# Attention in a hybrid layer: turned units rounded ahead of the exponentials, keys and values of a pair made in the shortest steps

## What is computed

```python
q = (rms_norm(c_q, q_norm_g) @ w_uq).reshape(B, S, 8, 64 + 32)       # then rope on the last 32
kv = (rms_norm(c_kv, kv_norm_g) @ w_ukv).reshape(B, S, 8, 64 + 64)   # k_nope, v; k_rope is shared by the heads
s = (einsum('bqhd,bkhd->bhqk', qn, k_nope) + einsum('bqhr,bkr->bhqk', qr, k_rope)) * scale
mask = key_chunk[None, :] <= q_chunk[:, None]                        # chunks of 64 positions
p = softmax(where(mask, s, -inf), axis=-1)
out = einsum('bhqk,bkhd->bqhd', p, v)
```

## Time and profile before

| | us |
|---|---|
| median of three runs (lowest to highest) | 2465.4 (2462.1 to 2468.1) |
| the profiled execution, its own time | 2465.6 |
| its span, first to last instruction | 2463.4 |
| PE busy in the span | 2246.3 |
| DVE busy | 1623.0 |
| ACT busy | 1220.3 |

### The profile page before, as it was taken

One profiled execution on the slowest core, in us unless ns is written; L12 is line 12 of the kernel. 1 busy time (PEld: TensorE's weight loads), 2 busy tenths in 40 slices (PEclk: granted clock), 3 DMA queues, 4 the chain that ended last, 5 costly groups with the idle time before them and its releaser, 6 DMA issues. The chain is left out here.

```text
span 2463.4 us, 42754 instructions
## 1 busy us (share of the span) xinstructions
PE 2246.3 (91%) x13522; PEld 1897.7 (77%) x13523; DVE 1623.0 (66%) x2948; ACT 1220.3 (50%) x2007; POOL 364.3 (15%) x255
## 2 busy tenths in 40 slices
PE   7999999998898999989979995899999999999970
PEld 6999989896777777777868885777777788888760
DVE  5445454556778778777756786687786765656646
ACT  4333333324666666666642220565665654454536
POOL 0000000000100001000001111123242322323216
PEclk9999999998999999999989996899999999999995
DMA  4122111251000000000134434698989978978837
GB/s 177 61 84 82 65 60 60 91 180 47 6 5 16 7 6 17 5 8 10 41 132 153 159 130 154 235 355 302 364 313 353 334 222 278 314 217 263 309 86 280
DMA packets 157242, 368.34 MB, mean 150 GB/s; under 512 B 25792, under 2 KB 37824, under 8 KB 155200
## 3 DMA queue, kind: packets, MB, share of 16 engines
q1 hardware_dynamic: 142592, 318.88, 35.5%
q0 software_dynamic: 13104, 47.72, 7.9%
q10 hardware_dynamic: 1440, 0.37, 0.1%
HBM read 295.11 MB, written 72.35 MB: 149 GB/s over the span
## 5 line engine op out<-in xcount | busy, mean ns | idle before, releaser
L2029 PE MATMUL eH<-w_hi,at_tok 128*128 128x512 f32 x720 | 288.8, 401 | 11.0 <-DVE at_tok L2147 11.0
L2080 ACT CAST w_hi<-w_raw 128x4096 fp32r (+1 forms) x64 | 232.7, 3636 | 109.6 <-DMA w_raw<-in_w 75.8
L2030 PE MATMUL eH<-w_hi,at_tok 128*128 128x512 f32 x720 | 286.3, 398 | 0.0
L2089 DVE TENSOR_TENSOR w_raw<-w_raw,w_hi 128x4096 f32 (+1 forms) x64 | 282.6, 4416 | 0.2 <-issue 0.2
L1224 DVE TENSOR_TENSOR prT_lo<-pT,prT_hi 128x512 fp32r<-128x512 f32 (+1 forms) x288 | 189.4, 658 | 97.6 <-ACT prT_hi L1104 97.5
L2089 DVE TENSOR_TENSOR w_raw<-w_raw,at_row 128x4096 f32 x32 | 141.6, 4426 | 125.1 <-ACT at_row L2080 125.0
L1104 ACT CAST prT_hi<-pT 128x512 fp32r<-128x512 f32 (+1 forms) x288 | 162.7, 565 | 120.6 <-PE pT L1008 119.9
L1142 POOL TENSOR_TENSOR qT_lo<-q_raw,qT_hi 128x512 fp32r<-128x512 f32 x32 | 41.0, 1280 | 1155.8 <-ACT qT_hi L1086 1155.8
L1215 DVE TENSOR_REDUCE mx<-pS 128x1 f32<-128x512 f32 (+2 forms) x320 | 188.5, 607 | 6.4 <-PE pS L998 1.2
L2034 PE MATMUL eH<-w_raw,at_tok 128*128 x720 | 183.9, 397 | 8.7 <-DVE w_raw L2089 8.6
L1096 ACT ACTIVATE pr<-pS,nmx 128x512 f32<-128x512 f32 (+1 forms) x240 | 154.0, 645 | 71.7 <-DVE nmx L1219 71.2
(11 more groups left out here) (369 smaller groups left out, 5680.6 us busy)
## 6 DMA issues: line engine op xcount, KB each, us to landing
w_raw<-in_w SPq DMA_DIRECT2D x96, 2048.0 KB, 13.8
xt<-in_x SPq DMA_DIRECT2D x9, 1024.0 KB, 8.1
xs<-in_x SPq DMA_DIRECT2D x8, 1024.0 KB, 5.1
scratch_h<-hp SPq DMA_DIRECT2D x16, 512.0 KB, 2.7
scratch_z<-hp SPq DMA_DIRECT2D x16, 512.0 KB, 3.6
fz<-scratch_z SPq DMA_DIRECT2D x16, 512.0 KB, 8.1
out<-fz SPq DMA_DIRECT2D x16, 512.0 KB, 2.6
scratch_xT<-xT_hi SPq DMA_DIRECT2D x7, 1024.0 KB, 3.9
```

The costliest lines, as they stand in the source:

```text
L2029: pe.matmul(H[:], xh[:, k, :], w.hi[:, k, :], start=(k == 0), stop=False)
L2030: pe.matmul(H[:], xl[:, k, :], w.hi[:, k, :], start=False, stop=False)
L2080: nc.scalar.copy(w.hi[:], w.words(o).bitcast(F32)).then_inc(w.hi_ready, 1)
L2089: v.tensor_tensor(w.words(o), w.words(o).bitcast(F32), w.hi[:].bitcast(F32), ALU.subtract).then_inc(w.lo_ready, 1)
```

## The change

Four edits, all in `phase_b` and its tables.

1. On ScalarE a half rounds two turned units (slots 0 and 1) before its first exponential, and from then on the casts run one ahead of the exponentials. Before, each cast was followed by an exponential.
2. Keys and values of the next pair are made in steps 14, 15 (of the odd head) and 0, 1 (of the pair's own even head): "k" in each first half, "v" in each second half, chunk 0 to 3.
3. Where the pieces and the preparations of a half are at most four together (`prep_leads`), the preparations come ahead of the slots: on PE right behind the scores, on VectorE right behind the maximum, on ScalarE behind the first exponential. This holds for all key and value chunks (those of pair 0 in steps 0 to 2 too) and for the query chunks of steps 1, 3, 5, 11, 13 and 15, not for those of 7 and 9.
4. The lo part of the very first query chunk is made by VectorE in the prologue and not by GpSimd.

```diff
-V_STEPS = {(3, 0): 0, (4, 1): 1, (6, 1): 2, (7, 0): 3}
+PAIR_STEPS = {(NQ + 6, 0): [("k", 0)], (NQ + 6, 1): [("v", 0)], (NQ + 7, 0): [("k", 1)], (NQ + 7, 1): [("v", 1)],
+              (0, 0): [("k", 2)], (0, 1): [("v", 2)], (1, 0): [("k", 3)], (1, 1): [("v", 3)]}
 
 
 def prep_in(n, i):
 
-    h, turn = STEPS_B[n][0], n % NQ
     out = list(FIRST_STEPS.get((n, i), []))
-    if h % 2 == 1 and h + 1 < HEADS:
-        if i == 0 and turn % 2 == 0:
-            out.append(("k", h + 1, turn // 2))
-        if (turn, i) in V_STEPS:
-            out.append(("v", h + 1, V_STEPS[turn, i]))
+    pair = (n + NQ) // (2 * NQ) * 2
+    if 0 < pair < HEADS:
+        out += [(kind, pair, c) for kind, c in PAIR_STEPS.get((n % (2 * NQ), i), [])]
...
+def prep_leads(n, i):
+
+    return PIECES[n][i] + len(prep_in(n, i)) <= 4
...
                         if n < NI:
                             score(n, i)
+                            if prep_leads(n, i):
+                                for p in prep_in(n, i):
+                                    project(p)
                         for s in slots_in(n, i):
...
-                        if n < NI:
+                        if n < NI and not prep_leads(n, i):
                             for p in prep_in(n, i):
                                 project(p)
...
-                        for k in range(max(len(slots), pieces)):
+                        for k in range(max(len(slots), pieces + 1)):
                             if k < len(slots):
                                 if slots[k] < NU:
                                     cast(slots[k])
                                 if slots[k] in COPY_SLOT:
                                     copy_o(COPY_SLOT[slots[k]])
-                            if k < pieces:
-                                exp(n, i, k)
-                            if k == 0 and n < NI:
+                            if 1 <= k <= pieces:
+                                exp(n, i, k - 1)
+                            if k == 1 and n < NI:
                                 for p in rounding:
                                     round_q(p)
+                                if prep_leads(n, i):
+                                    for p in prep_in(n, i):
+                                        copy(p)
                         if n < NI:
-                            for p in prep_in(n, i):
-                                copy(p)
+                            if not prep_leads(n, i):
+                                for p in prep_in(n, i):
+                                    copy(p)
...
-                for no in range(NQC):
+                pool.wait_ge(q_lo, 1)
+                for no in range(1, NQC):
...
                 for p in PROLOGUE:
                     ready(p)
+                    if p == q_chunk(0):
+                        v.wait_ge(q_hi, 1)
+                        v.tensor_tensor(ql[:, 0], qst[:, 0], qh[:, 0].bitcast(F32), ALU.subtract).then_inc(q_lo, 1)
                 for n in range(NI + 2):
                     for i in range(2):
                         if n < NI:
                             peak(n, i)
+                            if prep_leads(n, i):
+                                for p in prep_in(n, i):
+                                    ready(p)
```

More of the change, by code:

```diff
@@ L966, in project @@
                     at = slice(c * 512, (c + 1) * 512)
-                    if c == 0 and x == 0 and kind == "k":
+                    if c == 0 and x == 0:
                         pe.wait_ge(w_loaded[g], h // 4 * 48 + 48)
```

## The result

The changed kernel takes 2481.1 us in the median (2480.1 to 2483.8, four runs), the kernel before 2464.8 (2462.1 to 2468.1). The ratio is 1.0067 with a 95% interval of 1.005 to 1.0085: slower by 16 us. The forecast was 2480 us.

A forecast was written before the change was run, and what follows sets the result against it. It took a ring of waits among the in-order queues of PE, ACT and DVE to bound the attention stage. Terms -29 - 18 + 42 + 16 + 3 - 0.4 = +14 on 2465.6 gave 2480 us, range 2457 to 2500.

The forecast's parts named there:

- The short steps: Steps 30 to 33, which take in keys and values: 35.7 us where it was 20.2; +14 a pair, +42 us for three.
- the chain: In one half, maximum, exponential, copy, split of keys or values and splits of units follow one another; the next maximum waits behind.
- The 2.2 us for casts behind PE's projections: Step 14, key half: two casts wait for turns that stand behind the key matmuls on PE, 2.2 us on top of 5.6.
- Keys and values out of the long steps: Steps 40 to 45 and their like lose five key and value chunks: 6.1 us a pair, -18 us for three.
- The 7.0 of the windows: Steps 40 to 45 against 56 to 61: 10.5 us less, 3.5 of it two query chunks, the rest 7.0.
- The casts: Two casts before the first exponential: 0.4 us gained in each of 72 halves, -29 us.
- Leading query chunks: Query chunks ahead of the slots in steps 3, 5, 11, 13: +4 for each 16 steps, +16 us.
- Steps 0 to 2: Same chunks in the changed order, units on top of the chain in four halves and one more exponential: +3 us.
- First query chunk: POOL's subtraction of 1.28 becomes one of 0.7 on DVE, with the first maximum behind it: -0.4 us.
- The chain overlaps after all: Rival: copies early enough that DVE pays only its own work, short steps 5.8 a pair; 2439 us, chance 0.16.
- Casts worth twice as much: Rival: a half gains 0.6 to 0.7 and the sum is within 5 us of zero; 2467 us, chance 0.14.
- The clock: Rival: PE's clock falls in the emptier short steps, +4 us a pair; 2492 us, chance 0.18.

The follow-up runs named there:

- copies-first run: The changed kernel, but ACT copies leading keys and values at the very start of the half, before casts and exponential: 2439.6 us, ratio 0.9907.
- the move alone: Edits 2 and 4 on the kernel before; preparations at the end of a half, casts and exponentials in turns: 2472.2 us, ratio 1.0031.
- queries behind: The changed kernel, but a half that makes queries does its preparations at its end: 2468.5 us, ratio 1.0016.
- the lead: Edits 3 and 4 on the kernel before, with old places and old order of casts and exponentials: 2504.0 us, ratio 1.0164.
- casts first in the old places: The changed kernel with the old places of keys and values (edits 1, 3 and 4): 2520.7 us, ratio 1.0236.
- casts and the move: The changed kernel without edit 3, every preparation at the end of its half: 2451.3 us, ratio 0.9954.

## Why the prediction was right, point by point

**The short steps** were the heart and held: 35.7 us forecast, 36.4 measured. By halves: forecast 7.8, 4.0, 3.9, 4.3, 4.4, 2.9, 4.3, 4.1; measured 8.3, 3.8, 4.2, 4.4, 4.3, 2.9, 4.6, 4.0. What made this exact was that steps 0 to 2 of the kernel before already ran the chain, so that nearly each link had a row. The 2.2 us for casts behind PE's projections had none: it was an estimate, and in the trace the second cast ends 2.7 us after the maximum. I also expected DVE to wait 1 to 1.3 us in each half; it was 0.99 to 1.51 in seven and 4.28 in the first. That what stands ahead of the copy is the cost, and not something of the same size, is shown by the copies-first run.

**Keys and values out of the long steps:** forecast -6.1 a pair, measured -7.4 with the move alone. The 7.0 of the windows was nearer; I took off too much for query chunks.

**The casts** were mis-sized: -29 forecast, -16 measured. The 0.4 us a half is right only in the last head (steps 56 to 61: 5.1 us in their twelve halves). In the falling heads that also make keys and values it is 0.3 (steps 24 to 29: 3.5 us), and in the rising heads 0.3 us for six whole steps. I counted 18 alike halves of each 32, and left out that each exponential later keeps a bank from the next scores, which are more in rising heads; PE's wait for exponentials at its scores rose by 12.6 us. That this is why the rising heads gain nothing is argued from this wait and not shown. What is shown is that step 37 loses by step 36's order.

**Leading query chunks** were mis-sized the other way: +16 forecast, 1.9 and 0.8 us in each pair of heads measured, over four rising and three falling heads 10 us, and 5 more in steps 15 and 17 that I had within another term. Step 5 went as walked, first exponential 3.5 us after the end of the scores (I said 4):

```profile
990.83 0.16 DVE L1228 TENSOR_REDUCE mxa<-mx 128x1 f32<-128x3 f32 x1
992.71 0.48 ACT L1110 CAST prT_hi<-pT 128x384 fp32r<-128x384 f32 x1
993.09 0.69 ACT L1102 ACTIVATE pr<-pS,nmx 128x512 f32<-128x512 f32 x1
```

Now the order of the queues. The Trainium skill says what the walk assumed ("PSUM — Partial Sum Buffer", "Engine vs sequencer instructions"): the queues of ScalarE and VectorE are strict first in, first out. The trace agrees: in step 30 DVE stays idle until 929.19, ahead of the key split, though the casts of two units were done at 926.3 and 927.6.

**Steps 0 to 2:** +3 forecast, +3.1 measured. **First query chunk:** -0.4 forecast; the first maximum came 0.7 sooner.

With the measured sizes the sum is -16 - 3 x 7.4 + 3 x 16.3 + 10 + 3 - 1 = +23 for the attention stage, against 19.6 in the trace (the edits overlap; the query chunks of steps 15 and 17 stand in one term only) and 16 in the medians. So the forecast of +14 came closer to the medians than its terms deserve. It had 13 us too much gain for the casts and some 2 us too little loss for each pair's short steps; against that stood 6 us too much loss for the queries and 4 us too little gain in the long steps. These leave 9 us, and the rest went back where the edits overlap and in the stages behind. The sign rests on the short steps alone.

**The rivals.** "The chain overlaps after all" fell: 36.4 us, not 26. It was the right picture of the copies-first kernel, where the copies *are* early enough: 24.2 us. "Casts worth twice as much" fell. "The clock" came true in the trace, but not in the time: the granted clock was 0.95 in the short steps after where it had been 1.00, and 0.70 in steps 0 to 2 where it had been 0.81. All three short groups of the changed kernel had 0.95 (36.43, 36.43 and 36.44 us), so they can't price it; other runs can, and there the cost depends on where the low clock falls. In the kernel with queries behind the three short groups had 0.93, 0.85 and 0.90, and took 34.86, 34.86 and 34.87 us on DVE: nothing is felt. Where the move stands alone, its groups took 29.9, 31.0 and 30.9 us at 0.89, 0.84 and 0.83, and the whole difference lies in one half, the first of steps 15, 31 and 47. Two stretches of the first group and the same two of the second (PE's busy time and the granted clock):

```profile
762.00:766.00 4.00, 1.89 (x18) 1.75 (x17) 2.94 (x9) 2.07 (x6) 0.00 (x0) 1.00 0.01 1
766.00:770.00 4.00, 4.00 (x27) 3.20 (x27) 3.66 (x12) 2.53 (x7) 0.00 (x0) 1.00 0.00 0
925.00:929.00 4.00, 1.89 (x14) 1.75 (x13) 2.94 (x9) 1.61 (x6) 0.00 (x0) 0.85 0.00 0
929.00:933.00 4.00, 4.00 (x21) 2.99 (x21) 2.52 (x10) 2.78 (x7) 0.00 (x0) 0.72 0.00 0
```

In the second group the clock fell behind a gap of PE; the key matmuls of step 31 took 1.84 us and not 1.02, and ACT's copy waited 0.90 us for them. So the clock is worth about 1 us there, about a quarter of what I gave it for each pair. With the copies first it stays at 1.00:

```profile
904.10:927.50 23.40, 21.78 (x134) 16.58 (x133) 20.74 (x62) 18.28 (x49) 2.56 (x2) 1.00 0.03 7
```

The rule of the Trainium skill that I had cited ("TensorE: Matmul & The Clock Gate", "HAM oscillation — how this bites in real kernels": idle gaps bring the throttle back) agrees with these rows in part. The drop stands behind a gap, PE busy 1.89 of 4.00 us, but a gap of the same size in the first group had no drop behind it. Its price in this kernel is small by the six groups above.

## What to carry to other kernels

When work is put "where there is room", walk the in-order queues: ask of each instruction that is moved forward what its input waits for, and whether that input stands in the other engine's queue behind something that needs your own last result. Here a copy that needed nothing of the maximum stood behind an exponential that did; putting the copy first on its engine turned the same edit from 16 us lost into 23 to 25 us gained, and with the query chunks left behind into 37 to 39. A stretch that already runs the new pattern, however short, prices it better than any sum of busy times.

## What I had not expected

- Edits of order interact strongly: the lead cost +40 us alone, +74 with casts first in the old places and +28 with casts and the move. In the last case, with the copies first, it gained 12.
- The casts-first order gains most, for a step, where a half has only two units (step 13: 8.0 to 6.7 us on DVE).
- The stages behind the changed one differed by 4.9 us between the profiled executions of two kernels that are alike there, and by up to 10 us among the experiments.
